# Two neighbouring rows per partition in the down and output projections of a hybrid decoder trunk

## What is computed

```python
def swiglu(h, w_gate, w_up, w_down):
    return (jax.nn.silu(h @ w_gate) * (h @ w_up)) @ w_down

def hybrid_mixer(h, w_in, ...):
    proj = h @ w_in
    a, b, p, gc, gp = jnp.split(proj, IN_SPLITS, axis=-1)
    yc = conformer_conv(a, b, conv_dw, conv_dw_b, conv_ln_g, conv_ln_b, w_conv_out)
    yp = multiscale_pool(p, w_pool, pool_scale)
    merged = jax.nn.sigmoid(gc) * yc + jax.nn.sigmoid(gp) * yp
    return merged @ w_out

for layer in range(DEPTH):                      # DEPTH = 2
    h = rms_norm(x, mix_norm[layer])
    x = x + hybrid_mixer(h, w_in[layer], ...)
    h = rms_norm(x, ffn_norm[layer])
    if layer % 2 == 0:
        x = x + swiglu(h, dense_w_gate[i], dense_w_up[i], dense_w_down[i])
    else:
        x = x + moe_ffn(h, router_w[i], moe_w_gate[i], moe_w_up[i], moe_w_down[i])
return rms_norm(x, final_norm)
```

## Time and profile before

| | before |
|---|---|
| median of three runs | 1528.25 us (1527.32 to 1533.24) |
| span of the profiled execution (no other time of that execution is recorded) | 1530.0 us |
| TensorE, matmuls | 1483.3 us busy, 97% |
| VectorE | 1194.3 us, 78% |
| ScalarE | 993.4 us, 65% |
| GpSimd | 152.1 us, 10% |
| mean granted TensorE clock | 0.990 of full speed |
| read from memory | 432.73 MB, 284 GB/s over the span |
| packets on the load queue | 184704 |

### The profile page before, as it was taken

The page is one execution under the profiler, slowest core; times in us unless marked ns, Lnnn a source line. Parts: engine busy times, 40 slices in busy tenths (PEclk is TensorE's granted clock), DMA queues, the critical chain, the costliest instruction groups (busy, mean ns, idle before and its releaser), DMA issues.

```text
span 1530.0 us, 18439 instructions
## 1 busy us (share of the span) xinstructions
PE 1483.3 (97%) x6617; PEld 1199.5 (78%) x6617; DVE 1194.3 (78%) x979; ACT 993.4 (65%) x880; POOL 152.1 (10%) x236
## 2 busy tenths in 40 slices
PE   7989999999988899999999999999999999999997
PEld 5877888888866688788788878878878887887885
DVE  3867644456866788988898898898888889889886
ACT  5665544336764666767767677776776677767764
POOL 5860400000740000000000000000000000000000
PEclk9999999999999899999999999999999999999999
DMA  9535555555336499989989899998989989999890
GB/s 333 190 116 197 174 192 185 181 184 179 120 128 234 165 339 350 373 327 376 337 335 373 326 361 346 348 376 326 376 333 336 370 328 359 348 345 374 328 357 29
DMA packets 186223, 434.42 MB, mean 284 GB/s; under 512 B 7824, under 2 KB 11200, under 8 KB 186176
## 3 DMA queue, kind: packets, MB, share of 16 engines
q1 hardware_dynamic: 184704, 432.20, 77.2%
q10 hardware_dynamic: 1472, 1.61, 0.3%
HBM read 432.73 MB, written 1.05 MB: 284 GB/s over the span
## 4 chain that ended last, share of the span: by engine, by line
PE 82%; POOL 6%; DVE 4%; issue 4%; ACT 3%; DMA 1%; SPq 0%; POOLq 0%; DVEq 0%; ACTq 0%
PE bank L1123 26%; PE bank L1125 25%; PE bank L1124 25%; POOL work L465 4%; PE bank L1272 2%; DVE w_lo L780 1%; ACT w_hi L526 1%; POOL gates L421 1%; PE bank L1343 1%; DVE dT_lo L1047 1%; DMA xs<-in_x_dram 1%; PE bank L1368 1%; PE bank L1369 1%; PE bank L1351 0%; PE bank L1175 0%
## 5 line engine op out<-in xcount | busy, mean ns | idle before, releaser
L780 DVE TENSOR_TENSOR w_lo<-raw,w_hi 128x2048 fp32r<-128x2048 f32 x315 | 717.3, 2286 | 255.5 <-ACT w_hi L526 253.5
L526 ACT ACTIVATE w_hi<-raw 128x2048 fp32r<-128x2048 f32 x315 | 602.3, 1916 | 371.4 <-PE bank L1125 364.0
L1123 PE MATMUL bank<-w_hi,dT_hi 128*128 128x512 f32 (+1 forms) x912 | 364.7, 400 | 7.4 <-ACT gates L567 3.5
L1125 PE MATMUL bank<-w_hi,dT_lo 128*128 128x512 f32 (+1 forms) x912 | 359.1, 394 | 0.0
L1124 PE MATMUL bank<-w_lo,dT_hi 128*128 128x512 f32 (+1 forms) x912 | 359.0, 394 | 0.0
L1123 PE MATMUL bank<-w_hi,cT_hi 128*128 128x512 f32 x568 | 226.5, 399 | 0.0
L1125 PE MATMUL bank<-w_hi,cT_lo 128*128 128x512 f32 x568 | 224.3, 395 | 0.0
L1124 PE MATMUL bank<-w_lo,cT_hi 128*128 128x512 f32 x568 | 224.2, 395 | 0.0
L1123 PEld LDWEIGHTS bank<-w_hi,dT_hi 128*128 128x128 f32 x912 | 171.7, 188 | 50.3 <-issue 5.0
L1125 PEld LDWEIGHTS bank<-w_hi,dT_lo 128*128 128x128 f32 x912 | 171.5, 188 | 41.2
L1124 PEld LDWEIGHTS bank<-w_lo,dT_hi 128*128 128x128 f32 x912 | 171.8, 188 | 38.4
(11 more groups left out here) (189 smaller groups left out, 1283.5 us busy)
## 6 DMA issues: line engine op xcount, KB each, us to landing
raw<-in_moe_w_gate_dram SPq DMA_DIRECT2D x96, 1024.0 KB, 7.1
raw<-in_moe_w_up_dram SPq DMA_DIRECT2D x72, 1024.0 KB, 9.3
raw<-in_moe_w_down_dram SPq DMA_DIRECT2D x72, 1024.0 KB, 7.5
raw<-in_w_in_dram SPq DMA_DIRECT2D x28, 1024.0 KB, 5.3
mix<-in_moe_w_up_dram SPq DMA_DIRECT2D x16, 1024.0 KB, 9.0
gates<-in_moe_w_down_dram SPq DMA_DIRECT2D x16, 1024.0 KB, 9.4
gates<-in_moe_w_up_dram SPq DMA_DIRECT2D x16, 1024.0 KB, 8.6
work<-in_moe_w_down_dram SPq DMA_DIRECT2D x16, 1024.0 KB, 9.1
```

Source lines behind the costliest of these rows:

```text
L526: act.activation(w_hi[:, u % SPLIT, 0:width], place[slot][:, 0:width], ACT.Copy).then_inc(hi_ready, 1)
L780: dve.tensor_tensor(w_lo[:, u % SPLIT, 0:width], place[slot][:, 0:width], w_hi[:, u % SPLIT, 0:width].bitcast(F32), ALU.subtract).then_inc ...
L1123: nc.tensor.matmul(dst, a_hi, b_hi, start=start, stop=False)
L1125: return nc.tensor.matmul(dst, a_lo, b_hi, start=False, stop=stop)
```

## The change

A new function `pair_units` takes the place of `row_units` for w_out and for all down projections. It takes the same 256 rows of the matrix, but gives partition p the neighbouring rows 2p and 2p + 1, which lie behind each other in memory: one run of 8 KB. Block a of the unit thus holds the rows 2p + a. The activations that meet it must have the same index on partition p, so the transposes that feed these products take every second column: `pair_columns(source, f)` gives for piece f of a pair of pieces the columns 2p + f % 2. `transpose_x` gets a flag for that, set for the merged activations only. w_conv_out keeps its row units.

```diff
+    def pair_units(w, r0, blocks):
+
+        return [(2, D, lambda j=j: w[(r0 + j) * P:(r0 + j + 2) * P, :].rearrange("(p a) n -> p a n", a=2))
+                for j in range(0, blocks, 2)]
+
+    def pair_columns(source, f):
+
+        return source[:, (f // 2) * 2 * P:(f // 2 + 1) * 2 * P].rearrange("p (t a) -> p a t", a=2)[:, f % 2, :]
...
-        return units + row_units(w_conv_out[l], 0, CC) + row_units(w_out[l], 0, KD)
+        return units + row_units(w_conv_out[l], 0, CC) + pair_units(w_out[l], 0, KD)
...
-                units += row_units(d, (c - 1) * 4, 4)
+                units += pair_units(d, (c - 1) * 4, 4)
...
-        return units + half + row_units(d, (DC - 1) * 4, 4) + row_units(d, DC * 4, 2)
+        return units + half + pair_units(d, (DC - 1) * 4, 4) + pair_units(d, DC * 4, 2)
...
-        return units + row_units(d, (FC - 1) * 4, 4)
+        return units + pair_units(d, (FC - 1) * 4, 4)
...
-            def transpose_x(source, banks, waits):
+            def transpose_x(source, banks, waits, pairs=False):
...
-                                                   source[:, b, k * P:(k + 1) * P], ident[:, :])
+                                                   pair_columns(source[:, b, :], k) if pairs else source[:, b, k * P:(k + 1) * P],
+                                                   ident[:, :])
...
-                transpose_x(gate_c, MERGED_BANKS, merged)
+                transpose_x(gate_c, MERGED_BANKS, merged, pairs=True)
...
-                        last = nc.tensor.transpose(bank[banks + b][:, f * P:(f + 1) * P], tokP[:, b, f * P:(f + 1) * P], ident[:, :])
+                        last = nc.tensor.transpose(bank[banks + b][:, f * P:(f + 1) * P], pair_columns(tokP[:, b, :], f), ident[:, :])
```

## The result

Over 20 runs each, the changed kernel takes 1533.07 us (median; 1532.14 to 1535.91), the kernel before 1532.01 us (1527.19 to 1533.27). The ratio is 1.0018 with a 95% interval of 1.0010 to 1.0026: slower by 0.18%, some 2.8 us. The medians lie only 1.06 us apart because the times of the kernel before fall into two groups, seven from 1527.19 to 1528.85 and thirteen from 1530.54 to 1533.27, with the median in the upper one; the means are 2.7 us apart, as the ratio says. That is within the 0.5% that I called no change, but it is not zero, and the profiles show it with far more precision than the times do.

The account below looks back on a forecast made before the run. The prediction took TensorE's full stream in the expert stage as the bound, with loads hidden. From the median of 1528.25 us it added 0 for the loads and 0 for the transposes: 1528 us, range 1522 to 1540.

Parts of the forecast that it names:

- What bounds the kernel: Expert stage: TensorE full, 120.00 and 119.71 of 120 us; loads wait for buffers, a weight always lands before it is wanted.
- Part 1, the loads: 131 down and output loads in 8 KB runs: 16768 packets fewer, perhaps 0.3 us less per load, 0 in time.
- Part 2, the transposes: 300 transposes on TensorE reading every second column as weight load: taken as costing 0, at most 31.5 us.
- Both ends of the bound: Price of the 300 strided transposes: from 0 up to another 105 ns each, 31.5 us in all.
- The half-rate rival: Strided weight loads of the 300 TensorE transposes run at half rate: up to 31.5 us more, 1560 us; chance 0.09.
- Whatever a transpose gains or loses counts in full: Transposes stand in order in TensorE's stream, which bounds the kernel, so any change in their time reaches the span.
- four of them again in 0.42 us: Sign of no change: four transposes on TensorE still take 0.42 us; at half rate they would show 0.8 us.
- The load at 187 ns: TensorE's 128x128 load of split operands, 47 ns over 140; at that price, wholly exposed, the 300 transposes cost 14 us.
- The queue as the bound: 8 KB loads are slower and fill the load queue's free 8.8 us an item; 1614 us at 50% slower; chance 0.02.
- a gain from lighter traffic: Expert stage: cheaper loads speed TensorE by 0.6 us, 1525.6 us with saved waits; gain beyond 0.5% given chance 0.04.
- Runs cut again at 4 KB: Load queue: hardware splits the 8 KB runs, queue 1 keeps 184704 packets, time 1528 us; chance 0.04.
- The rival with a partial price: Strided weight loads on TensorE cost beyond 25 ns a transpose, short of half rate; 1542 us at 47 ns; chance 0.02.

## Why the prediction was wrong

*What bounds the kernel* was right. TensorE's stream holds the time, and the loads wait for buffers; no experiment on the loads moved the item's step by more than 0.02 us.

*Part 1, the loads.* The value of 0 was right, as was the packet count to the last packet. The size of the saving was too large: I read 0.6 us for 256 runs off two rows, expected half of it for each load, and with it a DMA share down to 0.90. It fell to 0.92, and the load of w_out took 4.8 us, not less than the 4.7 before. The 0.6 us itself was a fair price for the step I read it from: cut from 4 KB to 2 KB, w_out went from 4.7 to 5.3 us. What failed is carrying it over to the step from 4 KB to 8 KB, where the loads of w_out and dense_w_down both took 4.8 us after 4.7. Nor is the time to landing what the DMA engines spend: from 4 KB to 2 KB their share rose by 0.02, or 2.5 us for an item's 14 loads, 0.18 us each.

*Part 2, the transposes.* This is the step that failed: "I take 0". Where a transpose pays it measured 12.6 ns in the items and 12.7 in the dense stage, spread over all 300 some 10.7, together 3.2 us, 0.2%. Both ends of the bound held, and the value lies far nearer to 0 than to 105 ns, so the time stayed in the range and on the right side of 25 ns. But the term is clear of zero. The argument that led to 0 was of the wrong kind: I compared how much memory a load with a stride passes over with what the moving stream passes over. A stride of 4 passes over twice as much as one of 2 and its loads take 206 ns against 203, its item 126.269 us against 126.310, so the stretch of memory isn't what is paid for. The half-rate rival failed too: the sign I gave for it, loads over 200 ns, came, but its price did not.

Two readings on the way were wrong as well. "Whatever a transpose gains or loses counts in full" holds for 252 of the 300; the first group of each item and the first half of each output projection end in a wait that takes up the difference. And the 0.42 us for four transposes, from which I took 105 ns each, is of just such a group: it contains the wait for w_lo. An ordinary group takes 0.35 us, 88 ns a transpose. So the sign "four of them again in 0.42 us" came true in the changed kernel at the very place where I had read it, and would have shown no change.

The load at 187 ns was the better neighbour: the strided loads came out at 202, close to it. (Its stationary operand is spreadT and not a split one, but cT_hi and cT_lo take 187 to 188 ns too.) But its duration couldn't be taken as the price either. A load of 140 ns had a step of 109 in the long groups, one of 202 to 208 has a step of 120: loads overlap, and over 60 ns of duration are worth 11 to 13 ns of the stream. Taking the 47 ns of that row as exposed gave 14 us, four times too much.

The Trainium skill's rule in "Advanced Engine Details and Errata", SBUF Cachelines, said that two accesses to a 16-byte line keep full speed. For weight loads of float32 the trace doesn't agree: every second column (two accesses to a line) and every fourth (one) take 203 and 206 ns. The measured numbers decide.

*The rivals.* The queue as the bound, and a gain from lighter traffic, did not come: with 8 KB runs and plain transposes an item takes 126.007 us against 126.014. Runs cut again at 4 KB: no, 167936 packets. The prediction named the Trainium skill, "DMA: Bandwidth & Descriptors", SWDGE vs HWDGE vs iDMA, for packets of at most 4096 bytes as the preferred ones; nothing here shows a cost of going beyond, since w_out landed in 4.8 us against 4.7 and the down loads in work in 8.9 against 9.1.

*The chances.* The rival with a partial price was right in kind; I gave it 0.02, and only from 25 ns on. Below that I had let it merge with no change, which is fair for what a few runs can tell and not for what 20 can.

## What to carry to other kernels

Where an engine is full, an access pattern that costs it nothing in instructions still has to be priced for that engine; here a saving on a queue with slack was paid for on the one engine without any. Price an instruction in a full stream by the step from start to start, not by its duration, and see first whether a wait closes the step: one group in seven here was held by VectorE, and a price read there is too high for the instruction and shows nothing of a change to it. If a layout needs a permutation, put it into an instruction of an engine that has room: VectorE did it for 0.055 us an item, TensorE for 0.303.

## What the runs showed of the hardware

- A weight load of 128 float32 columns takes 140 ns when they are neighbours (for a transpose) and on average 199 to 210 ns with a stride of 2, 3, 4 or 8. In groups of sixteen, the step of a further transpose goes from 109 to 120 ns. Behind a matmul of 512 columns 3 ns of it are left.
- Runs of 4 KB in place of 2 KB brought w_out's load of 1 MB down from 5.3 to 4.7 us in the thin stages; runs of 8 KB brought nothing more (4.8).
- Executions of the kernel before lie up to 6 us apart (1527.19 to 1533.27), and profiles differ before the first item while the items' step is the same to 0.01 us: the kernel with 2 KB runs reached its first item's event at 583.26 us, the kernel before at 586.71, and both step by 126.0. In the mixers TensorE idles and its granted clock falls (0.83 between 420 and 440 us in the kernel before). So the step of a repeated event tells 0.05 us apart where the time of a run does not tell 3.
